# Sink layer with its projection in the order query half 0, keys, half 1, values; three K-tiles of the output projection among each core's last transposes; two latent output chunks split on GpSimd

## The reference

```python
for i in range(4):
    h = rms_norm(x, norm_mix[i])
    y = (dsa_mixer, swa_mixer, mla_mixer)[i % 3](h, ...)
    x = x + y
    x = x + square(relu(rms_norm(x, norm_mlp[i]) @ w_up[i])) @ w_down[i]
```

```python
q, k, v = split(h @ w_in, [1024, 256, 256])
q, k = rms_norm per head of 64, with gains
logits = q k / 8 + bias, masked to the window
m = max(max(logits), sink); e = exp(logits - m)
p = e / (sum(e) + exp(sink - m))
y = (p v over the heads) @ w_out
```

## Time and profile before

| | |
|---|---|
| runs | 1748.64, 1750.18, 1747.1 us; median 1748.64 |
| the profiled execution | 1752.53 us, its span 1750.6, mean granted clock of TensorE 0.983 |
| busy share of the span | TensorE 95%, DVE 65%, ScalarE 53%, GpSimd 12% |
| chain of waits, share by engine | TensorE 84%, DVE 7%, ScalarE 6%, issue 2%, GpSimd 1% |
| core of layer 0 | about 671 to 707 us |
| sink layer: kv block, first scores, out 0 | 909, 949, 980 us |
| latent layer: first block, core, out 0 | 1182, 1223, 1258 us |
| core of layer 3 | about 1509 to 1545 us |

### The profile page before, as it was taken

How to read it: one execution, slowest core, us unless ns; L and a number is a source line. 1 busy time by engine, 2 the same in 40 slices (tenths; PEclk the granted TensorE clock), 3 DMA queues, 4 the chain that set the end, 5 groups by cost and what they waited for, 6 DMA issues and landing times.

```text
span 1750.6 us, 27159 instructions
## 1 busy us (share of the span) xinstructions
PE 1657.6 (95%) x9666; PEld 1396.5 (80%) x9666; DVE 1135.9 (65%) x1958; ACT 933.9 (53%) x1570; POOL 209.1 (12%) x248
## 2 busy tenths in 40 slices
PE   7997999999999997999998999998899999799998
PEld 6877888887888775888886798887698888579887
DVE  5667554555877868676666656666766565866555
ACT  5462455645454567544455654448754446664443
POOL 3023520100000007110002000003000000600000
PEclk9998999999999999999999999999899999899999
DMA  8540056446555551465663256643265665245652
GB/s 274 146 133 13 3 168 181 156 150 203 165 188 173 176 166 49 157 193 192 189 183 125 92 181 192 192 153 115 79 219 185 192 192 152 73 143 183 190 188 78
DMA packets 158515, 270.32 MB, mean 154 GB/s; under 512 B 15244, under 2 KB 42331, under 8 KB 158427
## 3 DMA queue, kind: packets, MB, share of 16 engines
q1 hardware_dynamic: 156907, 263.35, 48.1%
q0 software_dynamic: 1504, 5.79, 1.0%
q10 hardware_dynamic: 16, 0.00, 0.0%
HBM read 268.04 MB, written 1.07 MB: 154 GB/s over the span
## 4 chain that ended last, share of the span: by engine, by line
PE 84%; DVE 7%; ACT 6%; issue 2%; POOL 1%; DMA 0%; DVEq 0%; SPq 0%; ACTq 0%
PE p_AC L2619 12%; PE p_AC L2621 12%; PE p_AC L2623 12%; PE p_UP L2619 6%; PE p_UP L2621 6%; PE p_UP L2623 6%; PE p_UP L2653 5%; PE p_TP L2653 5%; PE p_TP L2688 3%; PE p_TP L2655 3%; PE p_UP L2655 3%; ACT t_lg L1551 2%; ACT t_wh L1441 1%; DVE t_wl L2085 1%; PE p_UP L2640 1%
## 5 line engine op out<-in xcount | busy, mean ns | idle before, releaser
L2085 DVE TENSOR_TENSOR t_wl<-t_raw,t_wh 128x1024 fp32r<-128x1024 f32 (+2 forms) x521 | 607.4, 1172 | 458.6 <-ACT t_wh L1441 455.7
L1441 ACT ACTIVATE t_wh<-t_raw 128x1024 fp32r<-128x1024 f32 (+2 forms) x525 | 529.0, 1014 | 555.2 <-PE p_AC L2623 253.8
L2619 PE MATMUL p_AC<-t_wh,t_uTh 128*128 128x512 f32 (+1 forms) x612 | 190.7, 393 | 4.5 <-DVE t_uTl L2283 2.1
L2621 PE MATMUL p_AC<-t_wl,t_uTh 128*128 128x512 f32 (+1 forms) x612 | 189.6, 391 | 0.0
L2623 PE MATMUL p_AC<-t_wh,t_uTl 128*128 128x512 f32 (+1 forms) x612 | 189.3, 391 | 0.0
L2619 PE MATMUL p_UP<-t_wh,t_hT 128*128 128x512 f32 (+1 forms) x528 | 167.5, 399 | 4.2 <-DVE t_hT L2130 4.2
L2621 PE MATMUL p_UP<-t_wl,t_hT 128*128 128x512 f32 (+1 forms) x528 | 163.7, 392 | 0.0
L2623 PE MATMUL p_UP<-t_wh,t_hT 128*128 128x512 f32 (+1 forms) x528 | 162.8, 390 | 0.0
L2621 PEld LDWEIGHTS p_AC<-t_wl,t_uTh 128*128 128x128 f32 x612 | 115.5, 189 | 24.4
L2623 PEld LDWEIGHTS p_AC<-t_wh,t_uTl 128*128 128x128 f32 x612 | 115.5, 189 | 24.2
L2619 PEld LDWEIGHTS p_AC<-t_wh,t_uTh 128*128 128x128 f32 x612 | 112.6, 189 | 27.1 <-DVE t_uTl L2283 2.5
(11 more groups left out here) (367 smaller groups left out, 2720.6 us busy)
## 6 DMA issues: line engine op xcount, KB each, us to landing
t_raw<-in_w_up SPq DMA_DIRECT2D x128, 512.0 KB, 3.9
t_raw<-in_w_down SPq DMA_DIRECT2D x128, 512.0 KB, 3.9
t_raw<-in_w_in SPq DMA_DIRECT2D x72, 512.0 KB, 3.7
t_raw<-in_w_up SPq DMA_DIRECT2D x88, 256.0 KB, 4.0
t_raw<-in_a_w_in SPq DMA_DIRECT2D x24, 512.0 KB, 4.1
t_raw<-in_w_down SPq DMA_DIRECT2D x44, 256.0 KB, 3.2
t_raw<-in_a_w_out SPq DMA_DIRECT2D x16, 512.0 KB, 3.3
t_raw<-in_b_w_in SPq DMA_DIRECT2D x12, 512.0 KB, 4.0
```

Source lines behind the costliest of these rows:

```text
L1441: A_(wh[:, c % SPL, 0:size(c)], raw[:, c % RAW, 0:size(c)], ACT.Copy).then_inc(high_done, 1)
L2085: V.tensor_tensor(wl[:, c % SPL, 0:n], raw[:, c % RAW, 0:n], wh[:, c % SPL, 0:n].bitcast(F32), ALU.subtract).then_inc(split_done, 1)
L2619: M(outs[t], a_hi[t], w_hi[:, k, :], start=first and k == 0, stop=False)
L2621: M(outs[t], a_hi[t], w_lo[:, k, :], start=False, stop=False)
```

## The change

Four parts. (1) The sink layer's blocks become q0, keys (256 columns, two chunks of four K-tiles), q1, values. Within q1, TensorE transposes query half 0 behind the third chunk and the keys behind the fourth. The programs of ScalarE, DVE and GpSimd are put in the same order, the sums and the norm of half 1 come earlier. (2) In each core TensorE does the first three K-tiles of out 0 before the core's end (`begin_block`): in layers 0, 1 and 3 in steps 7, 8 (ahead of the transposes) and 10 (ahead of the last product); in the latent layer in steps 8 (ahead of them), 9 (behind them) and 10. The first waits until all maxima are taken. (3) `use` and `block_mm` learn to do part of a chunk. (4) In the latent layer GpSimd rounds and subtracts chunks 0 and 1 of out 0 behind its query norms; ScalarE and the DVE keep chunks 2 and 3.

```diff
@@ -279,4 +279,6 @@
                 v = rows(b_w_in_2[n])
-                b["kv"] = add_block(column_block(v, KD, 1024, 512))
-                b["q"] = two_blocks(v, 0)
+                b["q"] = [add_block(column_block(v, KD, 0, COLS))]
+                b["k"] = add_block(column_block(v, KD, 1024, 256))
+                b["q"].append(add_block(column_block(v, KD, COLS, COLS)))
+                b["v"] = add_block(column_block(v, KD, 1280, 256))
                 turn[0] = 0
@@ -518,5 +520,6 @@
         KIT, QC = {0: 1, 3: 7}, {0: 2, 1: 4, 3: 8}
-        HN = {0: (1, None, 2), 1: (3, 4, 5), 3: (6, None, 7)}
+        HN = {0: (1, None, 2), 1: (4, 3, 5), 3: (6, None, 7)}
+        HD = {0: (1, 2, 3), 1: (5, 4, 6), 3: (7, 8, 9)}
         HALF1_STEP = (1, 2, None)
-        HALF1_NORM = (0, 2, None)
+        HALF1_NORM = (0, 1, None)
         q_squares = slot(5, 1024, 1024).rearrange("p (t n) -> p t n", t=NT)
@@ -862,3 +865,3 @@
 
-            upto(dve, "hn_done", 3 * SI[layer] + 2 + half)
+            upto(dve, "hn_done", HD[layer][1 + half])
             for t in range(NT):
@@ -883,3 +886,3 @@
             def key_sums():
-                evacuated(dve, b["kv"])
+                evacuated(dve, b["kv"] if kind == 0 else b["k"])
                 ksq = slot(1, 128, 1536) if kind == 0 else slot(1, 512, 1024)
@@ -893,3 +896,3 @@
             def key_copies():
-                upto(dve, "hn_done", 3 * SI[layer] + 1)
+                upto(dve, "hn_done", HD[layer][0])
                 for t in range(NT):
@@ -969,14 +972,17 @@
             else:
-                ahead(q0)
-                key_sums()
+                ahead(b["k"])
                 rests(q1, 0, 1)
-                key_copies()
+                half_sums_dve(dve, V, link, q0, 0)
                 rests(q1, 1, 2)
+                key_sums()
+                rests(q1, 2, 3)
+                half_norm_dve(dve, V, layer, 0)
+                rests(q1, 3, 4)
+                key_copies()
+                rests(b["v"], 0, 2)
+                rests(out0, 0, 1)
                 upto(dve, "kt_ps", SI[layer] + 1)
                 V.tensor_scalar(slot(3, 1024), TP[:, :], gains[:, gk:gk + 1], None, ALU.mult).then_inc(sem("kc_ps"), 1)
-                rests(q1, 2, 4)
-                half_sums_dve(dve, V, link, q0, 0)
-                rests(out0, 0, 2)
-                half_norm_dve(dve, V, layer, 0)
-                rests(out0, 2, 3)
+                half_sums_dve(dve, V, link, q1, 1)
+                rests(out0, 1, 3)
 
@@ -1285,6 +1291,9 @@
 
-                def inside_q0(i):
+                def inside_q1(i):
                     if i == 2:
-                        upto(pe, "prep_done", SI[layer] + 1)
                         pe.wait_ge(t_split, 4 * t_mix[layer] + 4)
+                        query_transposes_pe(pe, transposes, layer, 0)
+                    if i == 3:
+                        upto(pe, "qc_done", QC[layer] + 1)
+                        upto(pe, "prep_done", SI[layer] + 1)
                         transposes([(TP[:, g * S + t * P:g * S + (t + 1) * P], dup[:, t, g, :])
@@ -1292,10 +1301,7 @@
 
-                def inside_q1(i):
-                    if i == 2:
-                        upto(pe, "kc_ps", KC[layer] + 1)
-                        query_transposes_pe(pe, transposes, layer, 0)
-
-                block_mm(b["kv"])
-                block_mm(q0, within=inside_q0)
+                block_mm(q0)
+                block_mm(b["k"])
                 block_mm(q1, within=inside_q1)
+                block_mm(b["v"])
+                upto(pe, "kc_ps", KC[layer] + 1)
             upto(pe, "qc_done", QC[layer] + 1)
@@ -1564,6 +1570,6 @@
                         A_(hTh[:, i - 3, :], acc((i - 3) % 2, S), ACT.Copy).then_inc(oh_done, 1)
-                    if n % 3 != 1 and PAIRS <= i < PAIRS + 2:
-                        c = i - PAIRS + (2 if n % 3 == 0 else 0)
-                        highs(blocks["out"][0], c, c + 1)
+                    if n % 3 == 0 and PAIRS <= i < PAIRS + 2:
+                        highs(blocks["out"][0], i - PAIRS + 2, i - PAIRS + 3)
                 if n == 2:
+                    act.wait_ge(high_done, item_chunks(blocks["out"][0])[1] + 1)
                     highs(blocks["out"][0], 2, 4)
@@ -1849,8 +1855,16 @@
                     else:
-                        read_block(b["kv"], lambda t: slot(2, 1024)[:, t * COLS:(t + 1) * COLS], COLS, r_tok)
-                        highs(q1, 0, 4)
+                        kv_half = lambda j: lambda t: slot(2, 256, t * COLS + 256 * j)
+                        ahead(b["k"])
+                        highs(q1, 0, 1)
                         query_block(0)
-                        highs(b["out"][0], 0, 3)
+                        highs(q1, 1, 3)
+                        read_block(b["k"], kv_half(0), 256, r_tok, split_next=False)
+                        highs(q1, 3, 4)
+                        highs(b["v"], 0, 1)
                         query_half(0)
+                        highs(b["v"], 1, 2)
+                        highs(b["out"][0], 0, 2)
                         query_block(1)
+                        highs(b["out"][0], 2, 3)
+                        read_block(b["v"], kv_half(1), 256, r_tok, split_next=False)
                         highs(b["out"][0], 3, 4)
@@ -2005,2 +2019,12 @@
                             .then_inc(sem("cq_done"), 1)
+                    for c in item_chunks(layer_blocks[layer]["out"][0])[0:2]:
+                        pool.wait_ge(raw_in(c), arrive[c])
+                        pool.wait_ge(spl_free, c - SPL + 1)
+                        pool.wait_ge(high_done, c)
+                        pool.tensor_copy(wh[:, c % SPL, 0:size(c)], raw[:, c % RAW, 0:size(c)]).then_inc(high_done, 1)
+                        pool.wait_ge(high_done, c + 1)
+                        pool.wait_ge(split_done, c)
+                        pool.tensor_tensor(wl[:, c % SPL, 0:size(c)], raw[:, c % RAW, 0:size(c)],
+                                           wh[:, c % SPL, 0:size(c)].bitcast(F32), ALU.subtract)\
+                            .then_inc(split_done, 1)
                 else:
@@ -2025,6 +2049,9 @@
                     q1_last = item_chunks(layer_blocks[layer]["q"][1])[3]
-                    norm_power(0, 32, nh)
                     if kind == 0:
+                        norm_power(0, 32, nh)
                         pool_rest(q1_last)
-                    norm_power(1, 0, 16)
+                        norm_power(1, 0, 16)
+                    else:
+                        norm_power(1, 0, 16)
+                        norm_power(0, 32, nh)
                     hb = AH * layer
@@ -2177,4 +2204,2 @@
                 for i in range(PAIRS + 4):
-                    if n % 3 == 1 and i == 1:
-                        half_sums_dve(dve, V, link, blocks["q"][1], 1)
                     if i == HALF1_NORM[n % 3]:
@@ -2224,3 +2249,5 @@
                         rests(blocks["out"][0], i - PAIRS + 1, i - PAIRS + 2)
-                    if n == 2 and PAIRS <= i < PAIRS + 4:
+                    if n == 2 and PAIRS + 2 <= i < PAIRS + 4:
+                        if i == PAIRS + 2:
+                            dve.wait_ge(split_done, item_chunks(blocks["out"][0])[1] + 1)
                         rests(blocks["out"][0], i - PAIRS, i - PAIRS + 1)
@@ -2600,9 +2627,12 @@
 
-            def use(c, it, outs, lh, ll, k0, first, last):
+            def use(c, it, outs, lh, ll, k0, first, last, part=None):
 
-                pe.wait_ge(split_done, c + 1 if it is None else it * 8 + (c + 1 - 8))
                 ch = chunks[c]
+                if part is None:
+                    part = range(ch.nk)
+                if part[0] == 0:
+                    pe.wait_ge(split_done, c + 1 if it is None else it * 8 + (c + 1 - 8))
                 w_hi = wh[:, c % SPL, 0:size(c)].rearrange("p (k n) -> p k n", k=ch.nk)
                 w_lo = wl[:, c % SPL, 0:size(c)].rearrange("p (k n) -> p k n", k=ch.nk)
-                for k in range(ch.nk):
+                for k in part:
                     if second_half[0] is not None and lh is hTh and (k0 + k) % 2 == 0:
@@ -2623,3 +2653,4 @@
                         ins = M(outs[t], a_lo[t], w_hi[:, k, :], start=False, stop=last and k == ch.nk - 1)
-                ins.then_inc(spl_free, 1)
+                if part[-1] == ch.nk - 1:
+                    ins.then_inc(spl_free, 1)
 
@@ -2658,2 +2689,14 @@
 
+            begun = {}
+
+            def begin_block(it, k):
+
+                _, c0, cs_, g = items[it]
+                if k == 0 and g >= 2:
+                    pe.wait_ge(blk_free(g), g // 2)
+                nk = cs_[0].nk
+                use(c0 + k // nk, None, [bank(g, t) for t in range(NT)], hTh, hTl, k - k % nk, k == 0, False,
+                    range(k % nk, k % nk + 1))
+                begun[it] = k + 1
+
             def block_mm(it, lh=hTh, ll=hTl, k_first=0, tail=None, within=None):
@@ -2670,3 +2713,4 @@
                 _, c0, cs_, g = items[it]
-                if g >= 2:
```

(20 more changed lines are left out.)

6 lines of the change are left out of this document (3 added, 3 removed).

## The result

| | before | after |
|---|---|---|
| median of 11 runs | 1749.12 us (1746.08 to 1750.39) | 1744.31 us (1742.49 to 1748.05) |
| profiled execution, span, mean granted clock | 1752.53, 1750.6, 0.983 | 1748.05, 1746.2, 0.983 |
| TensorE's waits for ScalarE's copies of a pair (L1561, now L1567) | 16.8 us in 14 waits | 8.7 us in 7 waits |
| layer 0: step 6's products to output block 1 | 20.11 us | 21.01 us |
| sink layer, the same | 19.29 us | 20.96 us |

The ratio is 0.9979 with a 95% interval of 0.9972 to 0.9987: faster by 3.7 us (2.3 to 4.9); the medians differ by 4.8. The forecast was 8.9 us won; 1744.31 lies in its range of 1736.5 to 1745.5, above the likeliest case. The sink layer is layer 1.

The account below looks back on a forecast made before the run. The prediction took TensorE as the bound (95% busy), so only its waits or low-clock work could yield. Sink layer 6.1, layers 0 and 3 0.7 each, sink tail 0, latent 1.4: 8.9 us off 1748.64 gives 1739.7, range 1736.5 to 1745.5.

Parts of the forecast that it names:

- Sink layer, projection: Sink layer's reordered blocks before its core: first scores start at 945.2 against 948.84, 3.6 us won, if nothing is late.
- Half 1: Second query half in the sink layer: earlier norm and transposes bring the whole gain there to 5.4 to 6.9 us.
- front: Sink layer, projection and half 1 together: worth 5.4 to 6.9 us, taken as 6.1.
- the 6.9 us: Sink layer: full gain of the front if a TensorE kept busy to 945 holds the high clock.
- Three K-tiles in layers 0, 1 and 3: Ends of these attention cores: layers 0 and 3 gain 0.7 us each, the sink layer nothing.
- Latent core: Latent layer: K-tiles fill a hole, GpSimd splits chunks 0 and 1; block ends at 1268.0 against 1269.4, 1.4 us won.
- the wait ahead of K-tile 4: Latent core: chunk 2 is ready at 1262.4 though K-tile 4 was due at 1261.2, a wait of about 1.2 us.
- rival E: Latent core: GpSimd's new instructions hold up DVE instructions reading two SBUF operands; 22.1 us lost, 1763 us; chance 0.05.
- B: Four core tails: K-tiles delay transposes, copies and products by their full length, tails give nothing; 1742.5 us; chance 0.12.
- A: Sink layer: norm of half 1 binds, delayed 3 us by ScalarE's splits or the power; front gives 3; 1742.8; chance 0.16.
- C: Sink layer: half 0 still scaled late behind the DVE's key work; front 1.5, tails nothing; 1747.1 us; chance 0.09.
- D: Whole kernel: more than forecast, high clock throughout and chunk 2 in time; 11.0 us won, 1737.6 us; chance 0.06.

Follow-up runs that it names:

- e2: The kernel before with the sink order alone, no early K-tiles and the old latent split: 1742.80 us, ratio 0.9966 to the kernel before.
- e11: The sink order plus the K-tiles of layers 0, 1 and 3 as in the change, latent layer as before: 1742.23 us, ratio 0.9970.
- e3: The changed kernel with K-tile 0 of layers 0, 1 and 3 moved behind step 7's transposes and products: 1740.53 us, ratio 0.9957.
- e12: The sink order with K-tile 0 of layers 0, 1 and 3 behind step 7's products, latent layer as before: 1737.63 us, ratio 0.9940.
- e10: The changed kernel with GpSimd's two latent subtractions of 1,024 columns each cut into halves of 512: 1744.02 us, ratio 0.9979.
- e4: The changed kernel with GpSimd's two latent subtractions of 1,024 columns each cut into quarters of 256: 1740.10 us, ratio 0.9953.
- e8: The change without the sink order, so K-tiles and GpSimd's split alone on the kernel before: 1748.10 us, ratio 1.0003.
- e14: The kernel of e12 run again with no edits: 1738.68 us, ratio 0.9948 to the kernel before.
- e9: The changed kernel without the K-tiles, TensorE's wait for the last maxima kept in layers 0, 1 and 3: 1746.57 us, ratio 0.9986.

## Why the prediction was wrong

- **Sink layer, projection (3.6 us forecast): right**, term by term. First scores 3.7 us earlier, nothing late, the value chunks in time.
- **Half 1 (front 6.1 in all): right**; 5.5 us in the trace, 5.9 us by e2. The transposes of half 1 took 1.97 us, the upper of the two values given. From 909 to 945 TensorE was busy throughout at a granted clock of 1.00; the core's own waits for the maxima then ended that (0.77 from 945). By the Trainium skill (TensorE: Matmul & The Clock Gate, What's actually happening) the low clock is the default and activity releases it: the first stretch agrees (1.00 from 909 to 945), and the 6.9 us that the prediction worked out by this rule did not come, since the clock fell again behind these waits.
- **Three K-tiles in layers 0, 1 and 3 (1.4 us forecast, by the runs nothing, perhaps 0.7 us lost): wrong in one step.** "From the wait on TensorE has no hole: 3 groups of transposes at 0.83, 4 of products at 0.78, 8 K-tiles at 1.36" priced all work behind the wait at the high clock. That TensorE has no hole there was right; that it works at the high clock was not. Where the clock held, the sum came out: in seven of the twelve such tails of layers 0 and 3 it did, at 19.44 or 19.45 us, 0.7 under the kernel before, and in four of the six of layer 1 (18.85 to 19.44, before 19.29). In the other seven of these eighteen the clock fell to half behind the hole, and each cost 1.3 to 1.7 us more. Seven times 1.5 over eighteen is 0.6 us a tail, about 1.75 a kernel: by this estimate the 1.4 us are gone on the average, which agrees with e11 and e2. The rows for it were in the prediction: two holes of 2.13 us with transposes of 1.94 behind them. It used them for the holes that the change removes and not for the three that it opens.
- **Latent core (1.4 us forecast, 1.6 to 2.1 us lost by the runs): wrong in what was left out.** "GpSimd now splits chunks 0 and 1 ... done by 1245, due at 1251" was right (done at 1239.3), and so was the wait ahead of K-tile 4 (1.2 forecast, 1.16). But the sum counted these 7.4 us as work beside, at no price, and put what they do to the DVE into rival E alone, at 22 us and one chance in twenty. The mechanism of E came, at 2.63 us and a low clock behind it. The size of the loss comes from comparisons: the change (0.9979, 0.9982) over e11 (0.9970) is 1.6 to 2.1 us, e3 over e12 3.0. In the rows it is 2.5 us where the old latent layer keeps its clock (46.3 against 43.82), and nothing where it does not (46.7). The profile of before that the prediction read was such a slowed one, and it did not see that. The 0.66 for two instructions should have become a term: there the same normalisation ran beside GpSimd additions of 0.46 to 1.18 us (L2049, L2050), and the subtractions put beside it in the latent core, at 2.39 us by the prediction itself, were several times as long. The DVE's stall went with the length of GpSimd's single instruction (3.54, 2.46, 1.6 us in the change, e10 and e4). By the Trainium skill (SBUF — State Buffer, Terms, on the shared port pair) the lock is exclusive for a whole instruction and the loser blocks; these runs agree, since the stall shrinks with the length of one instruction while GpSimd's whole time grows (7.4 to 9.5 us).
- **Sum.** 5.9 won in the sink layer, less 0.7 and 1.6 to 2.1, makes 3.1 to 3.6 us against 3.7 measured, but this is hardly a test: each step is a difference of neighbouring ratios. The test is e2 and e8, one part and the rest apart: 5.9 won and 0.5 lost make 5.4 us. The 1.7 us between that and 3.7 are within the intervals.
- **The rivals.** B named the right place, and its objection, that it asks for new holes on TensorE, was true: the holes were there, in front of the K-tile and not behind it. Its mechanism is wrong (e3). A and C did not come: the norms and the sink layer's chunks were in time. D asked for the high clock throughout and for chunk 2 of the latent layer in time, and neither came.

What stays open: why the clock falls behind one hole of 2.0 us and not behind the next of the same code. That it is not the length alone, nor the wait for the maxima, shows in holes that no kernel here changed, those ahead of the first products of a core (TensorE waits for ScalarE's copies): in the sixteen profiles the six transposes behind them ran slow (1.19 us or more in place of 0.89) 5 times in layer 0 (holes of 1.55 to 1.95 us), 5 times in the latent layer (always 1.95 or 1.96 us) and never in layer 3 (1.46 to 2.65 us).

## What to carry to other kernels

Work moved ahead on an engine's queue brings its wait along: put it behind the instructions that are ready sooner, even if it could start earlier, and let it fill the time behind them. Here the same K-tiles two places later won 3 to 4.5 us (e12 and e14 over e2) where they had won nothing (e11 over e2). A hole of 2 us on TensorE should be priced with a chance of half clock behind it (1.5 us here) wherever one is opened, not only where one is closed. Before a loss is read from two profiles, look whether one of them ran a stretch at the low clock that the other did not. And a GpSimd instruction given to "idle" time should be cut into short pieces if the DVE works beside it on two operands in SBUF: the DVE's stall goes with the length of a piece, not with the sum. Even so, in quarters the split only drew level with the old one; the gain came with chunk 2.

## What the runs showed of the hardware

- Behind the wait for the last maxima the granted clock fell to 1.2 GHz in 7 of 18 tails with a K-tile behind the wait and in 2 of 3 with none. Where the wait was under 1.5 us (e8 and e9, sink layer) it did not. In the 27 tails of the nine profiles without that wait it never did, though many have holes of 1.0 to 1.2 us. One such drop lengthens the tail by 1.3 to 1.7 us.
- In the holes ahead of the first products of layer 0, the latent layer and layer 3, of 1.46 to 2.65 us and the same code in all kernels, the clock fell 10 times in 48.
- GpSimd subtracts 1,024 columns in 2.4 to 2.7 us and rounds them in 1.0 to 1.5. A DVE product of four numbers a partition, 0.16 us elsewhere, took 1.03 us beside the subtraction and ended with it; the normalisation of a pair, 1.03 us alone, took 1.89 beside the rounding, 3.54, 2.46 and 1.6 beside subtractions of 1,024, 512 and 256 columns; the DVE's maxima, which read PSUM and SBUF, kept their 0.28 and 0.41 us beside it.
- Two profiles of one kernel can differ by more than the change under study: the change's tail of layer 1 took 20.96 us in one and 19.34 in the other.
